# Transformer block with a 32-expert mixture: the last expert quad's loads, matmul order and closing normalisation rearranged

## What is computed

```python
# x: (256, 1024), after the first layer norm; combine: 2 of 32 experts per token have a weight
h = silu(einsum('td,edf->tef', x, w_gate)) * einsum('td,edf->tef', x, w_up) * combine[..., None]
ffn = einsum('tef,efd->td', h, w_down)          # 32 experts, d 1024, f 256
out = layer_norm(2 ** 0.25 * x + ffn, ln2_g, ln2_b)
```

## Time and profile before

| | us |
|---|---|
| median of 3 runs | 398.46 (398.39 to 398.82) |
| the profiled execution, its own time | 397.12 |
| its span in the profile | 394.9 |
| TensorE busy | 362.9 |
| VectorE / ScalarE / GpSimd busy | 161.4 / 138.4 / 35.1 |
| moved from HBM | 131.25 MB |

### The profile page before, as it was taken

One profiled execution on the slowest core, in us unless ns is written; L12 is line 12 of the kernel. 1 busy time (PEld: TensorE's weight loads), 2 busy tenths in 40 slices (PEclk: granted clock), 3 DMA queues, 4 the chain that ended last, 5 costly groups with the idle time before them and its releaser, 6 DMA issues.

```text
span 394.9 us, 8066 instructions
## 1 busy us (share of the span) xinstructions
PE 362.9 (92%) x3339; PEld 287.3 (73%) x3339; DVE 161.4 (41%) x331; ACT 138.4 (35%) x243; POOL 35.1 (9%) x42
## 2 busy tenths in 40 slices
PE   7999999999999999999899999999399499299895
PEld 7999988999999999989757575756156357157542
DVE  2645679796366546454630203121530110111135
ACT  4643456654745444425523131313010212112012
POOL 7000000000000000001000005208620000000001
PEclk9999999999999999999999999999799789699999
DMA  8799884866848757779999999999999999999962
GB/s 277 223 317 370 304 293 157 317 219 208 311 165 299 267 174 275 232 288 426 426 383 426 425 427 424 407 412 428 429 421 421 427 424 426 427 426 424 411 228 106
DMA packets 51362, 132.75 MB, mean 336 GB/s; under 512 B 2898, under 2 KB 36706, under 8 KB 40068
## 3 DMA queue, kind: packets, MB, share of 16 engines
q1 hardware_dynamic: 51028, 132.14, 86.6%
q0 software_dynamic: 304, 0.17, 0.2%
HBM read 131.25 MB, written 1.05 MB: 335 GB/s over the span
## 4 chain that ended last, share of the span: by engine, by line
PE 67%; DMA 18%; SPq 8%; DVE 3%; issue 1%; ACT 1%; POOL 0%; DVEq 0%; ACTq 0%
PE bank L1138 30%; DMA gu<-in_w_up 13%; PE bank L1392 10%; PE bank L1272 6%; SPq L398 5%; PE bank L1426 5%; DMA dn<-in_w_down 4%; PE bank L1254 3%; PE bank L1342 3%; PE bank L1438 3%; SPq L416 2%; PE bank L1206 1%; DVE wl L786 1%; PE bank L1213 1%; SPq L403 1%
## 5 line engine op out<-in xcount | busy, mean ns | idle before, releaser
L786 DVE TENSOR_TENSOR wl<-raw,wh 128x1024 fp32r<-128x1024 f32 x54 | 65.9, 1224 | 57.1 <-ACT wh L603 57.0
L1392 PE MATMUL bank<-gu,xg 128*32 128x256 f32 x1024 | 63.8, 410 | 20.9 <-DMA gu<-in_w_up 20.2
L1138 PE MATMUL bank<-xh,wh 128*128 128x256 f32 x288 | 82.5, 286 | 0.1
L1138 PE MATMUL bank<-xl,wh 128*128 128x256 f32 x288 | 81.4, 283 | 0.0
L1138 PE MATMUL bank<-xh,wl 128*128 128x256 f32 x288 | 81.4, 283 | 0.0
L603 ACT ACTIVATE wh<-raw 128x1024 fp32r<-128x1024 f32 x54 | 56.6, 1056 | 58.6 <-PE bank L1138 30.2
L1392 PEld LDWEIGHTS bank<-gu,xg 128*32 128x32 f32 x1024 | 34.0, 118 | 47.5 <-issue 26.8
L1138 PEld LDWEIGHTS bank<-xh,wh 128*128 128x128 f32 x288 | 55.2, 192 | 2.4 <-issue 1.6
L1138 PEld LDWEIGHTS bank<-xl,wh 128*128 128x128 f32 x288 | 55.2, 192 | 0.1
L1138 PEld LDWEIGHTS bank<-xh,wl 128*128 128x128 f32 x288 | 55.2, 192 | 0.0
L1033 DVE TENSOR_SCALAR xg<-bank,gcol,bcol 128x128 f32<-128x128 f32 x32 | 10.9, 405 | 59.2 <-PE bank L1342 59.2
(11 more groups left out here) (218 smaller groups left out, 486.2 us busy)
## 6 DMA issues: line engine op xcount, KB each, us to landing
gu<-in_w_up SPq DMA_DIRECT2D x32, 1024.0 KB, 21.2
gu<-in_w_gate SPq DMA_DIRECT2D x28, 1024.0 KB, 17.4
dn<-in_w_down SPq DMA_DIRECT2D x25, 1024.0 KB, 17.2
raw<-in_w_in SPq DMA_DIRECT2D x40, 512.0 KB, 4.8
raw<-in_w_o SPq DMA_DIRECT2D x8, 512.0 KB, 4.3
gu<-in_w_gate SPq DMA_DIRECT2D x8, 512.0 KB, 8.4
dn<-in_w_down SPq DMA_DIRECT2D x6, 512.0 KB, 16.2
raw<-in_w_out_conv SPq DMA_DIRECT2D x4, 512.0 KB, 4.4
```

Of the source, the lines that this page charges most:

```text
L786: dve.tensor_tensor(wl[:, s, :].rearrange("p (k c) -> p k c", k=KC), raw[:, pair % NRAW, :].rearrange("p (k c) -> p k c", k=KC) [:, :, n % ...
L1138: mm = pe.matmul(dst, w[:, k, :], v[:, i, :], start=(i == 0 and w is h and v is high_in), stop=(i == len(ks) - 1 and w is l))
L1392: mm = pe.matmul(bank[6 - part][g, 0:DE], xg[:, k, g], w[:, e, part, k, :], start=(k == 0), stop=(k == KC - 1), skip_group_check=True)
```

## The change

Six edits, all in the last quad and the closing norm:

- SP loads the up matrix of the quad's fourth expert in two transfers of 0.5 MB, contraction pieces 0 to 3 and 4 to 7; the second has a semaphore of its own, `last_up_end`.
- TensorE does the last quad's up products in pairs of experts: experts 0 and 1 for all k, then experts 2 and 3 for all k, with the wait for `last_up_end` ahead of k = 4. Two filler products are left of twelve.
- The shift product into bank 7 stands behind `down(0)` rather than behind L1472. `scatter(0)` follows it, ahead of rows 0 of pieces 1 and 2. The last scatters go piece 1 for both tiles, then piece 2 for both tiles.
- VectorE takes the statistics in quarters of 256 columns, eight `bn_stats` in place of four.
- TensorE's scatter of piece 2 into a tile waits, by the new semaphore `third_stats`, until VectorE has read the third quarter of that tile: both are in one bank. A `engine_nop` on VectorE in each earlier round keeps the count.
- SP stores tile 0's second half first, then its first half.

```diff
             def load_last_gu(c):
                 for e in range(QE):
-                    sp.dma_start(gu[(NQ - 1) % 2][:, e, c, :, :],
-                                 (wg_v, wu_v)[c][:, (NQ - 1) * QE + e, :, :]).then_inc(last_gu_in[c][e], 16)
+                    for i in range(2 if c and e == QE - 1 else 1):
+                        ks = slice(i * KHALF, (i + 1) * KHALF) if c and e == QE - 1 else slice(0, KC)
+                        sp.dma_start(gu[(NQ - 1) % 2][:, e, c, ks, :],
+                                     (wg_v, wu_v)[c][:, (NQ - 1) * QE + e, ks, :]
+                                     ).then_inc(last_up_end if i else last_gu_in[c][e], 16)
...
-            for t in range(TT):
-                for h in range(2):
-                    cols = slice(h * HALF, (h + 1) * HALF)
-                    sp.wait_ge(result_done[t][h], 1)
+            for t, h in ((0, 1), (0, 0), (1, 0), (1, 1)):
+                cols = slice(h * HALF, (h + 1) * HALF)
+                sp.wait_ge(result_done[t][h], 1)
...
                 take_y(c)
+                dve.engine_nop().then_inc(third_stats, TT)
                 take_gathered(c + 2)
...
             for t in range(TT):
                 dve.wait_ge(added, first + t + 1)
-                dve.bn_stats(stats[:, t, 0, :], bank[2 * t][:, :])
+                for i in range(2):
+                    dve.bn_stats(stats[:, t, i, :], bank[2 * t][:, i * SEQ:(i + 1) * SEQ])
             take_y(last)
             dve.tensor_tensor(scaled, bank[0][:, :], lng[:, 0:HALF], ALU.mult).then_inc(scaled_done, 1)
             for t in range(TT):
-                dve.wait_ge(added, first + TT + (NY - 1) * (t + 1))
-                link(dve.bn_stats(stats[:, t, 1, :], bank[2 * t + 1][:, :]))
-                variance(t)
+                dve.wait_ge(added, first + TT + t + 1)
+                dve.bn_stats(stats[:, t, 2, :], bank[2 * t + 1][:, 0:SEQ]).then_inc(third_stats, 1)
+            for t in range(TT):
+                dve.wait_ge(added, first + 2 * TT + t + 1)
+                link(dve.bn_stats(stats[:, t, 3, :], bank[2 * t + 1][:, SEQ:2 * SEQ]))
+                variance(t, 4)
...
-                        for part in range(2):
+                        for part in range(1 if last_quad else 2):
                             if last_quad:
                                 for e in range(QE):
                                     pe.wait_ge(last_gu_in[part][e], 16)
-                                    if part and e < QE - 1:
-                                        stay_warm(WARM_LAST[e])
...
+                        if last_quad:
+                            pe.wait_ge(last_gu_in[1][0], 16)
+                            stay_warm(WARM_LAST[0])
+                            pe.wait_ge(last_gu_in[1][1], 16)
+                            for k in range(KC):
+                                ups(k, [0, 1])
+                            pe.wait_ge(last_gu_in[1][2], 16)
+                            pe.wait_ge(last_gu_in[1][3], 16)
+                            for k in range(KC):
+                                if k == KHALF:
+                                    pe.wait_ge(last_up_end, 16)
+                                mm = ups(k, [2, 3])
+                            mm.then_inc(gu_ps, 1)
...
                             for t in tiles:
+                                if last_quad and i == NY - 1:
+                                    pe.wait_ge(third_stats, TT * c + t + 1)
                                 pe.matmul(bank[2 * t + lo // HALF][:, lo % HALF:lo % HALF + hi - lo],
...
                         if last_quad:
                             down(0)
+                            pe.wait_ge(put_done, c + 1)
+                            pe.wait_ge(ln2_done, 2)
+                            pe.matmul(bank[7][:, :], ident[:, :], lnb[:, 0:HALF], start=True, stop=False,
+                                      skip_group_check=True)
+                            scatter(0)
                             down(1, [0])
                             down(2, [0])
-                            scatter(0)
                             down(1, [1])
                             down(2, [1])
-                            for t in range(TT):
-                                scatter(1, [t])
-                                scatter(2, [t])
+                            scatter(1)
+                            scatter(2)
...
-            pe.matmul(bank[7][:, :], ident[:, :], lnb[:, 0:HALF], start=True, stop=False, skip_group_check=True)
```

More of the change, by code:

```diff
@@ L112, in hybrid_block @@
         half_neg = sb("half_neg", [P, TT])
-        stats = sb("stats", [P, TT, 2, 6])
+        stats = sb("stats", [P, TT, 4, 6])
         moments = sb("moments", [P, TT, 2])
@@ L338, in hybrid_block @@
         added = sem("added")
+        last_up_end = sem("last_up_end")
+        third_stats = sem("third_stats")
         phase_a = ([("q", 0), ("q", 1), ("k", 0), ("k", 1), ("v", 0), ("v", 1)]
@@ L509, in _ @@
                 load_dn_cols(i, NQ - 1)
-            for t in range(TT):
-                for h in range(2):
-                    cols = slice(h * HALF, (h + 1) * HALF)
-                    sp.wait_ge(result_done[t][h], 1)
-                    sp.dma_start(out_v[:, t, cols], result[:, t, cols]).then_inc(out_done, 16)
+            for t, h in ((0, 1), (0, 0), (1, 0), (1, 1)):
+                cols = slice(h * HALF, (h + 1) * HALF)
+                sp.wait_ge(result_done[t][h], 1)
+                sp.dma_start(out_v[:, t, cols], result[:, t, cols]).then_inc(out_done, 16)
             sp.wait_ge(out_done, 16 * 2 * TT)
@@ L918, in _, with variance @@
                 y_low(JP - 1, m)
-            def variance(t):
-                link(dve.bn_aggr(moments[:, t, :], stats[:, t, :, :]))
+            def variance(t, parts):
+                link(dve.bn_aggr(moments[:, t, :], stats[:, t, 0:parts, :]))
                 dve.tensor_scalar(moments[:, t, 1:2], moments[:, t, 1:2], EPS, None,
@@ L933, in _ @@
                 link(dve.bn_stats(stats[:, t, 1, :], x1[:, t, HALF:DM]))
-                variance(t)
+                variance(t, 2)
             dve.wait_ge(x1T_ps, 4)
@@ L1398, in quad, with ups @@
                                 mm.then_inc(gu_ps, 1)
+                        def ups(k, experts):
+                            for e in experts:
+                                g = slice(SLOTS * e, SLOTS * (e + 1))
+                                mm = pe.matmul(bank[5][g, 0:DE], xg[:, k, g], w[:, e, 1, k, :],
+                                               start=(k == 0), stop=(k == KC - 1), skip_group_check=True)
+                            return mm
+                        if last_quad:
[11 more added lines that the diff above has]
+                            mm.then_inc(gu_ps, 1)
                         pe.wait_ge(pickw_done, 2 * c + 2)
```

## The result

| | before | changed |
|---|---|---|
| median, 6 runs each | 398.42 us (397.26 to 399.08) | 401.15 us (400.19 to 401.62) |
| ratio | | 1.0072, 95% interval 1.0053 to 1.0091 |
| profiled execution: own time, span | 397.12, 394.9 | 400.19, 397.6 |

The account below looks back on a forecast made before the run. Landing transfers bound the kernel to about 380 us, then the compute chain; +0.15 (front) +0.53 (quarters) -0.86 (end) = -0.18 us took 398.46 to 398.28, range 397.6 to 399.3.

Parts of the forecast that it names:

- D: Start of the last quad's `down(0)`, 377.47 us before; forecast at 377.35, 0.12 us earlier.
- The added transfer: Splitting the fourth up matrix adds a transfer to the load queue, claimed to cost 0.10 us, bounds 0 and 0.6.
- M to D: From SP's issue of the last quad's first down transfer to the start of `down(0)`; forecast to change by -0.12 us.
- The rival of the held queue: Added transfer holds the load queue, so all down pieces land 2.1 us later instead of 0.1; 400.3 us, chance 0.03.
- Pairs at the price of fours: Last quad's up products: a step of two experts costs what a step of four costs, 0.216 us, doubling the work.
- The wait that eats the gain: Before `down(0)`: of 0.65 us gained on `hT`, 0.22 is kept, since piece 0's fourth transfer lands at 377.2.
- Shift product and `scatter(0)`: Behind `down(0)`, the moved product lies on TensorE's path; the front part as a whole comes to +0.15 us.
- D to S: From the start of `down(0)` to the start of the scatter of piece 1; forecast to grow by 0.27 us.
- Quarters and the wait: Last scatters and quarter statistics: 0.43 us per quarter plus hand-overs, +0.53 us for tile 0's moments.
- The rival of costly quarters: VectorE's quarter statistics cost what halves cost, 0.70 us each; total +0.81, 399.27 us, chance 0.12.
- The end: Closing products after tile 0's rstd: the shift product leaves TensorE's back-to-back sequence, -0.86 us.
- The rival that VectorE would take it back: At the end, TensorE's saving uncovers VectorE's last `finish`, so the end stays as before, 398.5 us; chance 0.12.

Follow-up runs that it names:

- e2: Kernel before with 96 unused bytes behind the tile of the statistics, which moves the weight buffers off a multiple of 256; 400.69 us, ratio 1.0066.
- e3: The changed kernel, run again without alteration; 400.66 us, ratio 1.0055 to the kernel before.
- e4: Changed kernel with its wider statistics tile behind all others and 96 unused bytes in its old place, weight buffers at old addresses; 398.05 us, ratio 0.9998.
- e9: e4 with the fourth up matrix in one transfer again, pairs of experts kept; 398.34 us, ratio 1.0013 to the kernel before.
- e10: e4 with statistics by halves, scatters by tile and no wait on third quarters, as before; 397.33 us, ratio 0.9979 to the kernel before.
- e11: e10 with the fourth up matrix whole and both shift products together while TensorE waits for rstd; 397.26 us, ratio 0.9984 to the kernel before.
- e1: Kernel before with one harmless edit, the round's end loaded by TensorE with bounds asserted; 397.68 us against 397.95, ratio 0.9994.
- e8: Kernel before with one edit, the shift product into bank 7 directly behind the one into bank 4; 397.87 us against 397.63, ratio 0.9996.
- e12: Kernel before with small tiles packed and moved, weight buffers starting 256 bytes lower at a multiple of 512; 398.40 us against 398.14, ratio 1.0002.

## Why the prediction was wrong

**The step that failed: an edit that was not costed.** The sum takes the change edit by edit and has no term for the wider tile of the statistics, because it issues nothing. It moved the weight buffers off a multiple of 256 bytes, and loads that no edit touches came slower through a queue that is full for 190 us: 421 GB/s instead of 426 from 302 to 340 us, and from the issue at 196.72 to D 1.6 to 2.6 us more than before's 180.75, in every shifted profile. Measured: +2.6 us (e2), where the change as a whole measured +2.9 and, in e3, +2.2. The forecast's own reading, that up to 380 us only bytes that land earlier count, was right and should have led there: what reaches the rate of that queue is worth more than all six edits: 6 GB/s of 426 went with 2.6 us in e2, where the edits were put at 0.18. Its lower and upper bounds were bounds on durations and left out the pace.

**The added transfer** was taken at 0.10 us. M to D grew by 0.58 in the changed kernel, and e4 had 20.12, less than before's 20.66: at equal addresses the split costs nothing that the runs or the profiles show. From the issue at 196.72 to D it is 180.8 in e4, 180.6 in e9 without the split and 180.75 before. The rival of the held queue falls.

**Pairs at the price of fours:** right, 6.88 us against 2 x 3.46. Where the second pair's data were there in time (e3, e4, e10), the two pairs took 6.27 to 6.28, about three steps less: at the seam, 371.75 to 372.35 in e4, six to eight instructions mostly run at once, where up to four do before 371.5 and after 372.6. The forecast had no such overlap. The wait that eats the gain was named: in e4 TensorE stands 0.76 us on the transfer before `down(0)`. Of the 0.12 that the forecast gained at D nothing is to be seen: from issue to D the kernels with pairs at the old addresses (e4, e9, e10, e11) have 180.5 to 180.8 us, as have those without.

**Shift product and `scatter(0)`:** D to S +0.26, forecast +0.27. The agreement is in part luck of the profile compared with: with the shift product in front the changed order takes 6.67 or 6.68 in every profile, the old one 6.41 in before but 6.27 in e1, e8 and e12, which makes it +0.41.

**Quarters and the wait:** +0.64, forecast +0.53. A `bn_stats` of 256 columns takes 0.43 as taken from the copies. The missing 0.1 is the way from VectorE to TensorE, 387.91 to 388.05, 0.14 us where 0.05 was taken, and the longer combination (0.26 for 24 inputs instead of 0.21 for 12). The rival of costly quarters falls. Outside the span the forecast kept the 2.2 us of before; with quarters it is 2.6 to 2.8, a term that it put at nothing.

**The end:** -0.86, as forecast. The rival that VectorE would take it back did not come true here; with the statistics by halves the two end together (e10, e8).

**Offset and spread.** For the edits alone the forecast of -0.18 us agrees with e4: ratio 0.9998, -0.1 us, within 0.9 us to both sides, which is too wide to confirm its terms. The spread was underrated: three runs within 0.4 us had been shown; 34 runs of the kernel before on one chip lay between 396.4 and 400.5.

## What to carry to other kernels

A change of a tile's size is a change of all addresses behind it. In a kernel that a full load queue bounds, work out where the big buffers start, keep them at a multiple of 256 bytes, which was 0.5 to 0.9% faster here, and put tiles that may grow behind them. When a stretch that no edit touches is slower, compare the GB/s and the length of the same issues there before looking for a cause in the edits. And a statistic is cut into pieces only where the hand-overs (0.31 us to VectorE, 0.14 back) cost less than what the pieces hide: here they cost 0.64 us, with 0.4 more outside the span, and hid nothing.

## What the runs showed that was not expected

- Weight buffers 32, 64, 96 or 128 bytes off a multiple of 256 cost 0.86, 0.62, 0.66 and 0.54% of this kernel; a start 256 bytes lower costs nothing (e12, ratio 1.0002). Whether the order within these four is real is open, as is which buffer carries how much: only all of them together were moved.
- TensorE's granted clock fell to 0.50 for 3.4 us near 187 us in some executions and not in others, in code all of them share; it put the changed kernel's profile 1.0 us behind from there on, and cost 1.1 us in each of the five profiles that have it.
- The kernels with statistics by quarters took 0.4 us more outside the profiled span than all others; which part of the edit does it is open.
- In e10 and e11, the kernels with the statistics by halves and the shift product off the end, ScalarE and VectorE finish within 0.05 us of each other, so the next gain there needs both.
